# Block inversions in two linear-attention mixers: 8 by 8 diagonal blocks by forward substitution on VectorE instead of the first doubling levels on TensorE

## The reference, cut to what matters

```
# gated_deltanet
lmat = where(strict, einsum('bhnid,bhnjd->bhnij', kb, k) * decay, 0)
tinv = triangular_solve(eye + lmat, eye, lower=True)
u = tinv @ (v * beta);  w = tinv @ (kb * exp(gc))
# rwkv7_scan, one step
sa = einsum('bhvk,bhk->bhv', state, a_t)
state = state * w_t + sa * b_t + v_t * k_t
out = einsum('bhvk,bhk->bhv', state, r_t)
```

## Time and profile before

| | |
|---|---|
| median of three runs | 2999.3 us |
| profiled execution | 2997.34 us, span 2995.5 us |
| TensorE matmul busy | 2904.0 us (97%) |
| VectorE busy | 2062.6 us (69%) |
| ScalarE busy | 1366.1 us (46%) |
| GpSimd busy | 366.7 us (12%) |
| mean granted TensorE clock | 0.979 of full |

### The profile page before, as it was taken

One profiled execution on the slowest core, in us unless ns is written; L12 is line 12 of the kernel. 1 busy time (PEld: TensorE's weight loads), 2 busy tenths in 40 slices (PEclk: granted clock), 3 DMA queues, 4 the chain that ended last, 5 costly groups with the idle time before them and its releaser, 6 DMA issues.

```text
span 2995.5 us, 42748 instructions
## 1 busy us (share of the span) xinstructions
PE 2904.0 (97%) x16976; PEld 2543.8 (85%) x16976; DVE 2062.6 (69%) x3119; ACT 1366.1 (46%) x2050; POOL 366.7 (12%) x404
## 2 busy tenths in 40 slices
PE   7999999999999999999998999999799999999997
PEld 6888888888888888888887899888688888888886
DVE  6785787766776666656668977866477777657655
ACT  5452354455554445444445433422255444434434
POOL 2120011110111111001002111100011111101102
PEclk9998999999999999999999999999799999999998
DMA  5353333455555555555555422311155555555554
GB/s 207 134 167 109 119 127 120 141 169 187 189 187 189 190 190 188 191 190 189 190 179 191 148 92 80 114 55 57 50 176 185 189 189 190 190 190 190 190 178 153
DMA packets 132246, 476.13 MB, mean 159 GB/s; under 512 B 14672, under 2 KB 14928, under 8 KB 131792
## 3 DMA queue, kind: packets, MB, share of 16 engines
q1 hardware_dynamic: 132048, 473.40, 47.4%
HBM read 471.24 MB, written 2.10 MB: 158 GB/s over the span
## 4 chain that ended last, share of the span: by engine, by line
PE 92%; DVE 4%; ACT 2%; issue 1%; DMA 0%; POOL 0%; DVEq 0%; ACTq 0%; SPq 0%; POOLq 0%
PE ps L855 92%; DVE ringl L1837 1%; PE ps L858 1%; DVE U L1837 1%; ACT high L1379 1%; DVE U L1846 0%; DVE hr L1846 0%; ACT U L1379 0%; DVE xT L1837 0%; DMA ring<-in_w_dram 0%; POOL U L2519 0%; DVE hx L1837 0%; DMA xT<-in_x_dram 0%; ACT U L1390 0%; DVE yur L1837 0%
## 5 line engine op out<-in xcount | busy, mean ns | idle before, releaser
L855 PE MATMUL ps<-hr,high 128*128 128x512 f32 x4688 | 1516.6, 402 | 26.1 <-DVE ringl L1837 19.0
L1837 DVE TENSOR_TENSOR ringl<-ring,high 128x1024 fp32r<-128x1024 f32 x882 | 1078.6, 1224 | 449.5 <-ACT high L1379 449.2
L1379 ACT ACTIVATE high<-ring 128x1024 fp32r<-128x1024 f32 x882 | 916.5, 1041 | 672.0 <-PE ps L855 658.8
L855 PEld LDWEIGHTS ps<-hr,ringl 128*128 128x128 f32 x4688 | 884.3, 189 | 207.4 <-issue 2.0
L855 PE MATMUL ps<-hr,ringl 128*128 128x256 f32 x4688 | 924.8, 279 | 0.0
L855 PEld LDWEIGHTS ps<-hr,high 128*128 128x128 f32 x4688 | 725.5, 190 | 33.3 <-issue 23.6
L855 PE MATMUL ps<-yur,high 128*128 128x512 f32 x2176 | 684.9, 396 | 13.4 <-DVE yur L1837 7.1
L2519 POOL TENSOR_TENSOR U<-U,rs 128x256 f32<-128x256 f32 x293 | 272.3, 929 | 1897.0 <-DVE U L1837 1866.0
L1379 ACT ACTIVATE U<-ps 128x256 f32<-128x256 f32 (+3 forms) x494 | 180.5, 376 | 708.8 <-PE ps L855 648.0
L855 PEld LDWEIGHTS ps<-yur,ringl 128*128 128x128 f32 x2176 | 412.1, 189 | 92.6
L855 PE MATMUL ps<-yur,ringl 128*128 128x256 f32 x2176 | 432.6, 280 | 0.0
(11 more groups left out here) (161 smaller groups left out, 1188.8 us busy)
## 6 DMA issues: line engine op xcount, KB each, us to landing
ring<-in_w_dram SPq DMA_DIRECT2D x872, 512.0 KB, 3.3
ring<-in_w_dram SPq DMA_DIRECT2D x32, 256.0 KB, 3.3
xT<-in_x_dram SPq DMA_DIRECT2D x4, 512.0 KB, 7.4
out_dram<-hx SPq DMA_DIRECT2D x4, 512.0 KB, 3.0
cst<-in_cst_dram SPq DMA_DIRECT2D x1, 1754.5 KB, 14.1
yT<-in_lora_dram SPq DMA_DIRECT2D x1, 1024.0 KB, 7.2
U<-in_lora_dram SPq DMA_DIRECT2D x1, 512.0 KB, 4.4
posi<-in_pos_dram SPq DMA_DIRECT2D x1, 128.0 KB, 3.4
```

What stands on the lines that cost most here:

```text
L855: return e.matmul(out, l, r, start=start, stop=stop)
L1379: return e.activation(out, i, ACT.Copy, scale=scale)
L1837: return e.tensor_tensor(out, a, b, op)
```

## The change

- The first three steps of the doubling (2 by 2 blocks, levels 1 and 2) go. In their place VectorE masks L^T to its 8 by 8 diagonal blocks (`B8`), sums over the blocks to get each row's seven coefficients (`tensor_reduce`), spreads them (`rows_`), and TensorE multiplies `B8` with them (one float32 matmul of 196 columns), so that each partition has the coefficients of its block. Then VectorE does the forward substitution in 14 dependent small operations on 28 columns at most, and expands the result into XT (512 columns), which `turned` transposes to X.
- Levels 3 to 5 stay; behind level 5 two VectorE transposes of 32 partitions x 4 x 32 fill the one block of XT that is missing, in place of TensorE's transposes and ScalarE's copy. Level 6 takes L^T like the others; its second group has Y (64 columns) as the stationary operand and writes 64 partitions.
- RWKV's step `l`, GpSimd's copies and their semaphores go. The four matmuls of the state update become two, each over both heads' columns.
- The planner's tables are changed to match, and the constants are 632 columns shorter.

```
+            def invert(pc, vc_, take, X, XT, LT, Y, tag):          # TensorE
+                columns, rows_, _, _ = small_blocks(Y)
+                b = take(vc_, "x", 2, tag)
+                e.wait_ge(vc_.sem, vc_.after("blk", tag))
+                mm(ps[b][:, 0:196], C("B8"), rows_.rearrange("p i k -> p (i k)"), True, True).then_inc(...)
+                yield "blk"
+                for lev in range(3, 7):
+                    e.wait_ge(vc_.sem, vc_.after("x", lev - 1, tag))
                     for m in range(4):
+                        i = mm(half_of(B, s, 0, m), LT[:, m, :], cols_of(X, s, 0)[:, m, :, :], True, True)
...
+                        if lev < 6:
+                            i = mm(B[:, m, 0:64], XT[:, m, :], Y[:, m, 0:64], True, True)
+                        else:
+                            i = mm(B[0:64, m, 0:64], Y[:, m, 0:64], XT[:, m, 64:128], True, True)
-                    if lev == 5:
-                        b = take(ac, "invt", tag)
-                        for m in range(4):
-                            i = tr(ps[b][:, 128 * m:128 * m + 128], X[:, m, :])
...
-                    b = take(vc_, "l", q)                              # RWKV, TensorE
-                    for h in range(2):
-                        for c in range(2):
-                            t = mm(ps[b][:, 128 * m:128 * m + 128], AR[:, c, 0, :], Bt[:, h, 128 * c:128 * c + 128], True, True)
...
-                                for h in range(2):
-                                    t = mm(ps[b][:, 0:128], r_, src[:, h, :], n == 0, n == 3)
+                                both_heads = shaped(src.rearrange("p h n -> p (h n)"), 4, 64)[:, 0:4:3, :]
+                                t = mm(shaped(ps[b][:, 0:128], 2, 64), r_, both_heads, r_ is Br, r_ is Kr)
...
+            def invert(pc, vc_, rota, X, XT, LT, Y, tag):          # VectorE
+                tt(X, LT, rep(C("B8"), 4), MUL)
+                e.tensor_reduce(columns, X.rearrange("p m (b j) -> p m j b", j=8)[:, :, 1:8, :], AX.X, ADD)
+                tt(rows_, over(columns.rearrange("p m i -> p (m i)"), 7), rep(C("E8", 0, 7), 28), MUL)
+                e.tensor_copy(x, rep(C("E8"), 4))
+                yield "blk"
+                f = shaped(ps[b][:, 0:196], 4, 7, 7)
+                for k in range(7):
+                    tt(t_[:, :, k:7], f[:, :, k:7, k], x[:, :, k:k + 1].to_broadcast([128, 4, 7 - k]), MUL)
+                    tt(x[:, :, k + 1:8], x[:, :, k + 1:8], t_[:, :, k:7], SUB)
+                tt(XT.rearrange("p m (b i) -> p m b i", i=8), x.unsqueeze(2).to_broadcast([128, 4, 16, 8]),
+                   shaped(C("B8"), 16, 8).unsqueeze(1).to_broadcast([128, 4, 16, 8]), MUL)
+                turned(vc_, XT, X, "x", 2, tag)
+                yield "inv0"
                 (levels 3 to 6: mask to Y; subtract from X, at level 6 from XT; `turned` behind 3 and 4)
+                    if lev == 5:
+                        for a in (0, 64):
+                            o = e.transpose(XT[a:a + 32, :, a + 32:a + 64], X[a + 32:a + 64, :, a:a + 32])
```

The tables of costs (us) that the planner goes by:

```
-INVERSE = [(f"inv{lev}{x}", ("PE", 0.9), ("DVE", 0.45 if x == "a" or lev == 5 else 1.2)) for lev in range(1, 6) for x in "ab"] \
-    + [("invt", ("PE", 0.45), ("ACT", 0.6)), ("inv6a", ("PE", 0.9), ("DVE", 0.45)), ("inv6b", ("PE", 0.9), ("DVE", 0.45))]
+INVERSE = [("blk", ("DVE", 1.6), ("PE", 0.35)), ("inv0", ("DVE", 4.3))] \
+    + [(f"inv{lev}{x}", ("PE", 0.9), ("DVE", 0.45 if x == "a" or lev == 6 else 1.0 if lev == 5 else 1.2)) for lev in range(3, 7) for x in "ab"]
```

More of the change, by code:

```diff
@@ L669, in build @@
         names = [n for n, *_ in DELTA]
-        sides["cv"] = [(f"conv{j}", [("DVE", 3.0)], need(("dn", g, j, 1), *ready_) + ([("dn", (g - 1) * len(names) + names.index("inv0"))] if g else []))
+        sides["cv"] = [(f"conv{j}", [("DVE", 3.0)], need(("dn", g, j, 1), *ready_) + ([("dn", (g - 1) * len(names) + names.index("blk"))] if g else []))
                        for g in range(4) for j in range(3)]
@@ L1089, in deltanet @@
                     e.wait_ge(dact.sem, dact.after("lt", g))
-                    yield from invert(dpe, dact, ddve, dpool, take, EG, DT, Lm, LTm, Ym, g)
+                    yield from invert(dpe, ddve, take, EG, DT, LTm, Ym, g)
                     b = take(dact, "vn0", g)
@@ L1255, in rwkv @@
                             yield "p"
-                    b = take(vc_, "l", q)
-                    for h in range(2):
-                        for c in range(2):
[L1259 to L1264, removed]
+                    yield from invert(pc, vc_, take, X, XT, P1[:, :, 0:128], Y, q)
                     e.wait_ge(vc_.sem, vc_.after("x", 6, q))
@@ L1626, in deltanet @@
                     yield "vk"
-                    for lev in range(1, 7):
+                    for _ in range(1 + 2 * 4):
                         rota.take()
[L1629 to L1634, removed]
                     vn = VN.rearrange("p (h c) n -> p h c n", c=2)
@@ L1756, in rwkv @@
                     yield "rows"
-                    for _ in range(5):
+                    for _ in range(4 + 1 + 2 * 4):
                         rota.take()
[L1759 to L1766, removed]
                     for c in range(2):
@@ L2145, in deltanet @@
                     e.wait_ge(dpool.sem, dpool.after("kg", g))
-                    e.wait_ge(ddve.sem, ddve.last())
-                    first_x(ddve, dpool, EG, DT, Lm, Ym, g)
-                    yield "inv0"
-                    yield from invert(dpe, ddve, rota, EG, DT, Ym, g)
+                    e.wait_ge(dact.sem, dact.after("lt", g))
+                    yield from invert(dpe, ddve, rota, EG, DT, LTm, Ym, g)
                     rota.take()
@@ L2410, in rwkv @@
                             yield "p"
-                    b, _ = rota.take()
-                    e.wait_ge(pc.sem, pc.after("l", q))
-                    tt(L, shaped(ps[b][:, :], 4, 128), rep(C("SL"), 4), MUL).then_inc(vc_.sem, vc_.inc("l", q))
-                    yield "l"
-                    e.wait_ge(vc_.sem, vc_.last())
-                    first_x(vc_, qc, X, XT, L, Y, q)
-                    yield "inv0"
-                    yield from invert(pc, vc_, rota, X, XT, Y, q)
+                    yield from invert(pc, vc_, rota, X, XT, P1[:, :, 0:128], Y, q)
                     for c in range(2):
@@ L2589, in deltanet @@
                     yield "o"
[L2591 to L2595 removed]
             weave(main(), [Side(n, places["POOL"][n], g) for n, g in (
[L2598 removed]
+                ("dn", deltanet()),)])
         @block.sync
@@ L2662, in constants @@
     K = np.arange(64)[None, :]
-    put("SL", (I > J).astype(np.float32))
-    put("MC", np.concatenate([I // 2 ** l == 2 * (K // 2 ** l) + 1 - t for l in range(7) for t in range(2)], 1).astype(np.float32))
+    put("MC", np.concatenate([I // 2 ** l == 2 * (K // 2 ** l) + 1 for l in range(3, 7)], 1).astype(np.float32))
+    put("B8", (I // 8 == J // 8).astype(np.float32))
+    put("E8", (I % 8 == np.arange(8)[None, :]).astype(np.float32))
     put("causal", np.where(J <= I, 0, NEG).astype(np.float32))
```

105 lines of the change are left out of this document (42 added, 63 removed).

## The result

| | before | after |
|---|---|---|
| median, same chip | 2998.8 us (4 runs) | 2952.05 us (4 runs, 2951.94 to 2952.28) |
| ratio | | 0.9844, 95% interval 0.9827 to 0.9861 |
| span of the profiled execution | 2995.5 us | 2950.0 us |
| TensorE idle in it (span less busy) | 91.5 us | 102.5 us |
| mean granted TensorE clock | 0.979 | 0.978 |

What follows compares the result with a forecast made beforehand. TensorE was taken as the bound, busy 2904 of 2995.5 us. 14 us from the delta rule and 34 from RWKV made 48 off 2997.3: 2949.3, or 2951 us on the median's level; eight-in-ten range 2934 to 2975.

Steps and rivals of the forecast that it cites:

- TensorE's work: Matmuls and transposes dropped from inversions, step `l` and state update, less the added product: 55.2 us, 40 in RWKV.
- Level 6's second group: Inversion matmuls with a 64-column stationary operand: taken at 0.222 us, no change; bound 5 us more gained.
- The small operations: VectorE's 14 substitution operations in each inversion: 0.18 us and a gap each, 3.1 us together.
- The reduction: VectorE's sum over 448 columns in the coefficient step `blk`: 0.62 us, bounds 0.5 to 0.9.
- the 5 to 15 named as a sign: Sign that the forecast holds: VectorE's busy time rises by 5 to 15 us.
- The delta rule's stage: Four inversions take 15 us off TensorE; 14 us of it shorten the time, gaps at the halts staying.
- stream 1's chain: Serial RWKV rounds of the stream that ends last: 33 us shorter over four rounds, rounds 8 us closer.
- The state update's work: RWKV's state update with two matmuls fewer in each of eight: 8 x 2 x 0.217 = 3.5 us off TensorE.
- Rival B: VectorE becomes the RWKV stage's bound, which gives only 20 us: 2965 us, range 2960 to 2990; chance 0.20.
- Rival A: All TensorE work and some waits go, including 5 us idle at RWKV's end: 2934 to 2940 us; chance 0.20.
- Rival C: Substitution step `inv0` delays VectorE's split, TensorE waits at each inversion: slower, 3010 us at 5.5 us each; chance 0.06.
- Rival D: Planner's new orders in the two stages bring 50 us of waits, time stays at 2999 us; chance 0.04.

Runs made afterwards that it cites:

- e12: Changed kernel with the coefficient step's mask writing its product reordered, so the reduction reads neighbouring elements; same order: 2955.25 us, ratio 0.9861.
- e1: Kernel before with the new inversion in the delta rule alone, RWKV as before: 2978.81 us, ratio 0.9940.
- e4: Changed kernel with only the first of the substitution's seven steps, 12 of 14 small operations left out (wrong result), order unchanged: 2948.8 us, ratio 0.9835.
- e11: e4's kernel with the planner's cost of `inv0` lowered from 4.3 to 1.8: 2939.57 us, ratio 0.9803.
- e3: Kernel before with the RWKV state update alone as two matmuls, planner's `o0` cost on TensorE lowered from 1.8 to 1.35: 2988.34 us, ratio 0.9967.
- e7: Changed kernel with the state update's four matmuls and their planner cost put back, the new inversion kept in both mixers: 2963.37 us, ratio 0.9880.
- e6: Kernel before with only the planner's `o0` cost on TensorE changed from 1.8 to 1.35, no work changed: 2991.04 us, ratio 0.9972.
- e9: e8's kernel with the planner's cost of `inv0` raised from 4.3 to 7.2: 2978.51 us, ratio 0.9933.
- e8: Changed kernel with each of the substitution's seven products done three times, 14 more small operations an inversion, order unchanged: 2999.7 us, ratio 1.0001.
- e10: Changed kernel with only the planner's cost of `blk` raised from 1.6 to its measured length, 2.2: 2956.11 us, ratio 0.9863.

## Why the prediction was right, and where it was off

**The time** (2951.0 for 2952.05) was right in part by luck: the delta rule gave 17.5 us for 14, the stretch behind the RWKV stage 3.3 for nothing, the RWKV stage 24.6 for 34.

**TensorE's work.** 55.2 us reckoned, 56.5 measured as busy time, and this too is closer than its parts: 3.4 lie in the stretch behind the RWKV stage, where no instruction went and TensorE is idle 18.8 us before and after, and the RWKV stage gave 35.5 of 40. There the mean granted clock fell from 0.95 to 0.93. As TensorE runs at one of two levels, 1.2 and 2.4 GHz, these rows give an estimate of 17 us more at the lower one, where successive records of 64 columns start 0.213 us apart for 0.112 at the upper (medians); so up to some 8 us of the work taken out may have come back as slower products. Level 6's second group was reckoned at no change. Its records start 0.059 us apart at the median, for 0.112 with the full stationary operand; eight of each in the changed kernel:

```profile
1843.19 1.00 PE L855 MATMUL ps<-U 128*128 128x64 f32 x8
1868.89 0.68 PE L855 MATMUL ps<-U 128*64 128x64 f32 x8
```

96 records make 5.1 us, the bound that the prediction had. That a stationary operand of half the columns costs half is what the Trainium skill's rule (TensorE: Matmul & The Clock Gate, LDWEIGHTS) gave, 5 us by its figure: the trace agrees. The new product's two records start 0.165 to 0.170 us apart in seven of the twelve, which fits the 0.33 taken for it, 0.24 in four, and 0.33 in the one at the lower clock.

**VectorE's step.** The small operations were sized right (0.166 to 0.182 us for 0.18), and `inv0` came to 4.3 us for 4.6. The reduction was mis-sized: 1.01 us for 0.62, outside its bounds; it reads every eighth element, and e12 shows that the same width read from neighbours takes 0.62. The block transposes took 0.303 each, just above the 0.2 to 0.28. VectorE's busy time rose by 16.6 us; the sum of 18 counted the gaps, and the 5 to 15 named as a sign was too low.

**The delta rule's stage.** All of TensorE's 15 us came off and 2.5 more, in e1 as well. Level 6's second group accounts for 1.7 of them (32 records at 0.053); where the rest comes from was not tried.

**RWKV, the step that failed.** The prediction took 34 us for the stage, from 40 of TensorE's work and 33 of stream 1's chain, "both limits fall nearly alike". The chain was the mis-sized term. From the X of round 1 (before 1738.30 in the earlier trace rows, after 1724.89) to that of round 7 (2088.41, and 2056.32) stream 1 is 18.7 us shorter, where the prediction's own terms give 27 for these three rounds; the rounds are 0.4, 12.4 and 5.9 us closer, not 8 each. Part of it is round 7, whose coefficients and substitution take 11.3 us from the mask to X and not 7, since the product between them comes late in TensorE's order:

```profile
2052.64 0.19 DVE L1806 TENSOR_TENSOR U<-ps,U 128x28 f32<-128x28 f32 x1 [4.44 <-PE ps L855]
...
2056.32 0.71 DVE L2003 STREAM_TRANSPOSE U<-U 128x512 f32<-128x512 f32 x1
```

The prediction added up the chain of a round as if the places of the steps came with it. They are set by the planner, and in the new order TensorE's idle time in the stage grew by 11 us, where the prediction left 6 of the work's 40 for that and for the chain together. 4.3 of it lie at the stage's end, which the prediction had unchanged, and 6.3 in mid-stage, where main work is missing: a substitution lies bare for 4.4 us, and the waits for the normalizations, 5.4 us before, are a little longer. e4 shows that the 4.4 follow the substitution's length: with 2.5 us less of it and the same order, the wait is 2.5 shorter. With a shorter step that the planner knows (e11) the place is full. Why the planner leaves it without main work was not tried. The state update's work was priced right (3.3 for 3.5) but brought 6 to 10 us with its new order (e3, e7), as e6 shows for the order alone; without that luck e7's 18.6 us and the work's 3 would have been the stage's gain.

**Rival B** (VectorE's capacity bounds) had nearly the right size for the stage, 20 us, by a wrong mechanism: with 20 us of VectorE's work taken out of the stage and the order kept, e4 is only 3.8 us shorter there, and e9, with e8's work on VectorE, is 20 us faster than e8 by its order alone. What is left of it is that VectorE's time in the rounds' chain does cost (e8 and e9; for e11 the order may be enough). **Rival A** fell: the idle time at the stage's end did not shrink but grew by 4 us. **Rival C** was priced too mildly and put in the wrong place. It supposed cover of 8.4 us through the split ahead, slack of 3 us, and break-even at 4.6 us an inversion above the forecast. There is no such cover at level 3: e8 breaks even at 2.9 us above the measured step, by waits for X and a lower clock, and the waits for the split stay at 19.5 us. Had the planner's 4.3 been 2.9 us short of the real step, the change would have gained nothing. **Rival D**'s remark that the planner lays every order anew was true, at the scale of 8 us and not of 50.

What stays open: how much of RWKV's shortfall a better placement could get back with the step at its real length. e10 is one other order, and it isn't better.

## What to carry to other kernels

Where orders are fixed from a table of costs, a step that exceeds its entry can be waited for nearly in full (`inv0` in e8; `blk`, 0.6 us above its entry, was not), and one that falls below it can give almost nothing until the table is told (e4, e11): change a step and its entry together, and measure the step in the trace before trusting either. When small matmuls are removed, look first at the stretches in which they were the only thing TensorE had: the new order may leave another engine's step bare there, as it did here. And a change in such a table alone can move the time by as much as a real saving (8 us here), so an edit's worth is read by making it with the order kept as well.

## What the runs showed of the hardware

- A VectorE reduction of 448 float32 elements takes 1.008 us when it reads at steps of 32 bytes and 0.620 us with neighbours; a product of 512 takes 0.69 us with a packed result and 1.04 with steps of 64 bytes in its result. The Trainium skill (Vector Engine (DVE) Microarchitecture Reference, Measured stream behaviour on trn2) says that a stream runs at full rate only in runs of at least two adjacent words, on the read or on the write side: both runs agree.
- Behind the RWKV stage, with the same instructions and after a wait of about 3.2 us, TensorE's clock fell for some 10 us before (second row) and not after; the remaining stretch is 849.1 and 845.8 us long.

```profile
2186.36:2196.36 10.00, 6.94 (x40) 5.87 (x38) 7.85 (x12) 5.08 (x7) 0.00 (x0) 0.95 0.60 198
2196.36:2206.36 10.00, 9.90 (x42) 8.54 (x43) 5.23 (x10) 3.31 (x7) 0.00 (x0) 0.71 0.23 62
```
```profile
2144.21:2154.21 10.00, 6.84 (x41) 5.83 (x39) 7.85 (x12) 5.26 (x7) 0.00 (x0) 1.00 0.61 194
2154.21:2164.21 10.00, 10.00 (x57) 8.75 (x58) 7.39 (x14) 4.88 (x8) 1.10 (x1) 1.00 0.37 117
```

The other profiles lie between 845.4 us (e10) and 849.5 (e6, e12), and e12 has TensorE's order of the changed kernel. So 3.3 us of the profile's 45.5 are no work that the change took out; what decides whether the clock falls there wasn't tried.
